# Seven filler products a round on TensorE in the RWKV-7 recurrence of a streaming encoder step

## The reference, cut to what matters

```python
def step(S, inp):
    r_t, w_t, k_t, v_t, a_t, b_t = inp
    sa = jnp.einsum('bhij,bhj->bhi', S, a_t)
    S = S * w_t[:, :, None, :] + sa[..., None] * b_t[:, :, None, :] + v_t[..., None] * k_t[:, :, None, :]
    y = jnp.einsum('bhij,bhj->bhi', S, r_t)
    return S, y
```

## Time and profile before

| | |
|---|---|
| median of 3 runs | 2306.42 us (2304.41 to 2319.5) |
| the profiled execution, its own time | 2300.22 us |
| its span, from the first to the last instruction | 2298.4 us |
| mean granted TensorE clock | 0.925 |
| TensorE busy | 2064.6 us, 90% of the span |

### The profile page before, as it was taken

The page is one execution under the profiler, slowest core; times in us unless marked ns, Lnnn a source line. Parts: engine busy times, 40 slices in busy tenths (PEclk is TensorE's granted clock), DMA queues, the critical chain, the costliest instruction groups (busy, mean ns, idle before and its releaser), DMA issues.

```text
span 2298.4 us, 37193 instructions
## 1 busy us (share of the span) xinstructions
PE 2064.6 (90%) x15388; PEld 1915.2 (83%) x15388; DVE 1332.8 (58%) x2123; ACT 747.0 (32%) x1290; POOL 198.3 (9%) x199
## 2 busy tenths in 40 slices
PE   2989988888888979899999998998778989999996
PEld 2988876667667759899999998998557989999996
DVE  7665566666666434876427745343554687526754
ACT  3443443333333322422112214222664422212222
POOL 2000223220222000000000000001320000000000
PEclk9999878777878859999999999999999999999998
DMA  2211000000000022122222122242542122222121
GB/s 111 91 66 44 11 1 13 12 7 8 13 11 12 12 96 76 45 85 72 69 88 74 61 68 74 83 151 91 212 150 76 72 74 70 69 83 74 67 69 58
DMA packets 30325, 150.69 MB, mean 66 GB/s; under 512 B 4784, under 2 KB 7600, under 8 KB 17872
## 3 DMA queue, kind: packets, MB, share of 16 engines
q1 hardware_dynamic: 30160, 148.32, 18.6%
HBM read 137.84 MB, written 10.47 MB: 65 GB/s over the span
## 4 chain that ended last, share of the span: by engine, by line
PE 58%; DVE 7%; ACT 3%; issue 2%; DMA 0%; DVEq 0%; ACTq 0%; POOL 0%; SPq 0%; POOLq 0%
PE ps L593 16%; PE ps L594 16%; PE ps L595 16%; PE ps L1936 1%; PE ps L1907 1%; PE ps L659 1%; PE ps L658 1%; PE ps L657 1%; DVE prob L2085 1%; ACT prob L1978 1%; ACT prob_t L1988 1%; DVE w_lo L588 1%; PE ps L1317 1%; PE ps L1916 1%; DVE split_f L804 1%
## 5 line engine op out<-in xcount | busy, mean ns | idle before, releaser
L593 PE MATMUL ps<-x_hi,w_hi 128*128 128x320 f32 x2208 | 692.8, 314 | 67.3 <-DVE x_lo L711 41.3
L594 PE MATMUL ps<-x_lo,w_hi 128*128 128x320 f32 x2208 | 689.5, 312 | 0.0
L595 PE MATMUL ps<-x_hi,w_lo 128*128 128x320 f32 x2208 | 688.9, 312 | 0.0
L593 PEld LDWEIGHTS ps<-x_hi,w_hi 128*128 128x128 f32 x2208 | 421.1, 191 | 72.4 <-issue 46.9
L588 DVE TENSOR_TENSOR w_lo<-raw,w_hi 128x2048 fp32r<-128x2048 f32 (+2 forms) x110 | 229.7, 2089 | 410.1 <-ACT w_hi L582 410.1
L594 PEld LDWEIGHTS ps<-x_lo,w_hi 128*128 128x128 f32 x2208 | 421.3, 191 | 0.2
L595 PEld LDWEIGHTS ps<-x_hi,w_lo 128*128 128x128 f32 x2208 | 421.0, 191 | 0.0
L582 ACT ACTIVATE w_hi<-raw 128x2048 fp32r<-128x2048 f32 (+2 forms) x110 | 192.0, 1745 | 419.6 <-PE ps L595 419.6
L593 PE MATMUL ps<-hid_hi,w_hi 128*128 128x320 f32 x704 | 217.5, 309 | 0.0
L594 PE MATMUL ps<-hid_lo,w_hi 128*128 128x320 f32 x704 | 217.5, 309 | 0.0
L595 PE MATMUL ps<-hid_hi,w_lo 128*128 128x320 f32 x704 | 217.5, 309 | 0.0
(11 more groups left out here) (263 smaller groups left out, 3121.6 us busy)
## 6 DMA issues: line engine op xcount, KB each, us to landing
raw<-in_w_gate SPq DMA_DIRECT2D x22, 1024.0 KB, 4.8
raw<-in_w_up SPq DMA_DIRECT2D x22, 1024.0 KB, 4.8
raw<-in_w_down SPq DMA_DIRECT2D x16, 768.0 KB, 4.2
raw<-in_w_down SPq DMA_DIRECT2D x16, 640.0 KB, 3.9
raw<-in_w_kv SPq DMA_DIRECT2D x8, 1024.0 KB, 4.8
past_k<-in_past_k SPq DMA_DIRECT2D x8, 1024.0 KB, 4.8
past_v<-in_past_v SPq DMA_DIRECT2D x8, 1024.0 KB, 4.9
raw<-in_w_r SPq DMA_DIRECT2D x4, 1024.0 KB, 6.9
```

What stands on the lines that cost most here:

```text
L593: pe.matmul(out, w, x, start=start, stop=False)
L594: pe.matmul(out, w, xl, start=False, stop=False)
L595: return pe.matmul(out, wl, x, start=False, stop=stop)
```

## The change

`pe_filler` is new: one float32 product of the identity with the first 256 columns of `table` into the first half of a bank. It is issued once for each of the chunks 1 to 4, after both banks of that chunk have been claimed and ahead of its score products, and once for each of the three groups of transposes, after its bank has been claimed. The products that follow have `start=True` and overwrite what the filler has left, before `fill` tells the reader. No semaphore is added, moved or taken away, and no other engine's program is changed. In the tile with the number f that makes 4 + 3 = 7 fillers, 56 over rounds 0 to 7.

```diff
@@ -1206,6 +1206,10 @@
             if tile_of(i - 1):
                 pe_states(pe, i - 1, k)
 
+    def pe_filler(pe, bank, n=2 * P):
+
+        pe.matmul(ps[:, bank, 0:n], ident, table[:, 0:n], start=True, stop=True)
+
     def pe_logits(pe, f):
 
         pe.wait_ge(S("low_wa2_in"), 16 * (f + 1))
@@ -1236,6 +1240,8 @@
         for u in range(u0, u1):
             at = slice(u * P, (u + 1) * P)
             banks = [claim(pe, ("gram", f, hh, u)) for hh in range(2)]
+            if u:
+                pe_filler(pe, banks[0])
             for hh, bank in enumerate(banks):
                 rows = slice(hh * HD, (hh + 1) * HD)
                 pe.matmul(ps[:, bank, 0:P], ra[rows, f % 2, A_OF, at], bk[rows, 0, at], start=True, stop=True)
@@ -1258,6 +1264,7 @@
 
         for j in range(3):
             bank = claim(pe, ("bk_tok", f, j))
+            pe_filler(pe, bank)
             for n in range(2 * j, min(2 * j + 2, NT)):
                 for q in range(2):
                     at = (n % 2 * 2 + q) * P
```

## The result

Nine runs of the changed kernel took 2318.97 to 2331.21 us, median 2327.86; nine of the kernel before beside them 2296.94 to 2319.5, median 2304.41. The ratio is 1.009, with a 95% interval of 1.0068 to 1.0112: by the ratio the change costs about 21 us; the two medians are 23.5 us apart. That is a cost of about 1%, and 2327.86 lies in the forecast's range of 2287 to 2333, 15 us above its 2313. The profiled execution took 2318.97 us (span 2317.2) against 2300.22 (2298.4) before; it is the fastest of its nine.

What follows compares the result with a forecast made beforehand. In the recurrence TensorE was taken as the busiest engine, through its low clock, and still waiting. Onto the profiled 2300.2 us came 16.1 of queue delay less 3.4 returned by the clock, 12.7 net: 2313 us, range 2287 to 2333.

Steps and rivals of the forecast that it cites:

- The price: Fillers' queue delay in the recurrence: round 0 2.4 us, rounds 1 to 6 1.7 each, round 7 3.5; sum 16.1.
- the two credits for the clock: Half clock in the scores removed by fillers: 1.7 us back in round 5, 1.7 in round 7, together 3.4.
- the 0.5 I took: Delay covered by TensorE's wait for ACT's bonus at the second transposes: 0.5 us or so, up to 0.95.
- The relay doesn't absorb: Sign of being wrong: the merging's relay absorbs the delay, leaving the distance from L1219 to L1317's later groups unchanged.
- my other sign of being wrong: Half-clock stretches summed over the recurrence, about 268 us, move by more than 20 us.
- The lottery: Shifting the merging against the clock's changes draws its half-clock stretches anew: about 6 us a round, sign unknown.
- case 1: Forecast for the whole kernel: queue delay paid, a little returned by the clock; 2313 us, 2304 to 2323; chance 0.50.
- the third case: Slower rival: nothing returned by the clock, round 6 loses its good draw, others worsen; 2322 or 2330 us, chance 0.20.
- The lock: Rival: round length is set by when the clock rises, so the delay disappears in half clock; 2300 to 2306, chance 0.13.
- The rule of the Trainium skill: Closing idle gaps between bursts keeps the clock up; the earlier trace agreed for round 5, not rounds 1 to 4.

Runs made afterwards that it cites:

- the shift: Kernel before the change, no filler, plus a TensorE wait for ACT's reading of the last transposed keys before the merging; median 2317.58 us, ratio 1.004.

## Why the prediction came out as it did

**The price.** The sum was 16.1 us, or 12.7 with the two credits for the clock. The first parts of the rounds have grown by 2.9 and 2.8 us in rounds 0 and 1, by 2.1 in rounds 2, 3, 4 and 6, by 1.0 in round 5 and by 1.4 in round 7: 16.4 in sum, in which the smaller half clock of rounds 5 and 7 is already counted. The term that was mis-sized is that of the fillers ahead of the scores. Three of them at 0.45 made 1.35, and they took 0.60 + 0.43 + 0.73 = 1.76, with 0.1 more ahead of the bonus; the transposes' price was right (0.43). Against that the waits covered more than the 0.5 I took, so that L1311 of round 2 starts 16.75 us behind L1223 where L1304 started 14.68 behind L1219: 2.07 us later, within the 1.75 to 2.2 counted in the prediction, of which the forecast then took no more than the low end, 1.7. What I had not priced is the passage between row shapes, though the trace of before had it: the weight load of L1228, the first 128-row product behind 64-row ones, starts after 0.33 us without one:

```profile
378.96 0.84 PEld L1228 LDWEIGHTS ps<-e_neg,table 128*128 128x128 f32 x4 [0.33 <-issue]
```

**The credits.** Their sizes came: round 5's first part has 2.8 us at half clock instead of 6.8, round 7's 2.9 instead of 8.2. Their cause isn't shown. With the transposes' fillers alone, so with none in the gap before chunk 2, the two have 2.9 and 2.9 as well; with the shift and no filler they have 7.2 and 8.3.

**The relay doesn't absorb.** Right: behind the round's first product the first group of L1317 started at 16.85 us in rounds 2 to 4, that of L1324 starts at 18.75, and the second groups at 22.8 and 24.7. The whole half clock in the recurrence, my other sign of being wrong, moved from 267.7 us (250 to 860) to 255.2 (250 to 880), within the 20 allowed.

**The lottery.** Its size, some 6 us a round, was right, and that it is drawn anew with the place of the work fits the table and the shift without a product. Its draw wasn't even. In the profiled execution the second parts cost only 2.2 us more in sum, and that is luck: round 6 lost its good draw (54.3 to 58.8), round 5 went from 60.5 to 64.5, round 1 from 56.5 to 59.6, and rounds 2 to 4 gained 2.5 to 3.1 each. Most other executions of the changed kernel had a mean clock of 0.922 or 0.923 for this one's 0.926; three or four thousandths of 2328 us, twice, are 14 to 19 us more at half, an estimated 7 to 9 us of time, and the median lies 8.9 above 2319. They have no trace, so where it lies isn't shown. The measured 2327.86 thus lies above case 1's own range (2304 to 2323) and within the third case (2322 to 2330), which had 0.20. So the forecast's mechanism, the price in the queue, held for 16.4 of the profiled execution's 18.8 us, and its number was too low by two things: the price of the score fillers, and the distance of the profiled execution from the others, 4.2 us before and 8.9 after, which I left to the range. That the other executions drew worse places is my reading and not shown.

**The lock** (case 4) was not there: round 2 went from 75.0 to 74.6 us, round 3 from 75.0 to 74.3, round 4 from 77.9 to 76.9, and rounds 5 and 6 grew by 4.9 and 6.7. Rounds 2 and 3 alone would look like it.

**The rule of the Trainium skill** ("TensorE: Matmul & The Clock Gate", section "HAM oscillation"), by which closing gaps keeps the clock up, would have given a gain. The page's case has waits for DMA between bursts, longer than any wait in these scores (2.6 us at most). In the scores of the changed kernel the runs show no gain that could be put down to the closed gap. In the merging they agree: eleven fillers a tile that stand in the waits there went with a clock of 0.89 for 0.78 in the recurrence and with 40 us less time. The change had the means in the wrong place: the scores of round 2 ran at 1.00 already.

What stays open: why some rounds fall 8.4 to 9.7 us behind the output transposes and others only at 18.3 to 19.0. The score fillers alone never had the early fall, the transposes' fillers alone had it three times in five. Why the score fillers alone gain 0.4 to 1.1% is open with it.

## What to carry to other kernels

In this kernel fillers paid where two things met: TensorE waited there anyway, and the clock fell behind it. Read both from the trace (waits by line, stretches at half clock) before placing one, and give it the row shape of its neighbours. In a kernel whose clock alternates, compare parts of the work at either level and not only the total: here the score fillers alone cost 1.1 us a round where they stood and the total fell by 0.7%. One trace is one draw, so look also at where its execution lies among the others.

## What the runs showed of the hardware that I had not expected

- A 128-row product of 256 float32 columns between groups of 64-row products took 0.73 us of TensorE's queue, between 128-row ones 0.43, and two of 64 rows side by side 0.33 between 64-row ones, all at full clock. At most changes of row shape the next weight load came after 0.33 us without one.
- In the nine kernels in which its work was the same, the stretch from a round's first output transpose to the next round took 51.9 to 65.1 us, with 12.4 to 44.6 us of it at half clock; six such stretches of five kernels with the same place agreed to a tenth of a microsecond (53.4).
- In the run that adds idle time of less than a microsecond ahead of the merging, and no product, two rounds had 46 us at half clock in the second part, the most of any run; in each the longest stretch lasted 37.5 us. Round 5 of the same run had 15.7.
